# Head 0 of the expert search: eight indices found from the best eight of each side ahead of the whole search

## Chip, cores and metric

The kernel runs on one core of one Trainium2 chip. The metric is the device time of one execution in microseconds, as the median of several runs. One execution was also taken with the hardware profiler; the rows below come from that one.

## What is computed

One transformer layer on 512 tokens of width 1024 in float32: a mixer of two kinds of attention, and then a retrieval of single-neuron experts (PEER). The part that the change touches is the retrieval. For each token and each of 8 heads it takes the 16 best keys on each of two sides, the 16 best sums of the 256 pairs, and gathers the experts' rows from two tables of 16384 rows:

```python
def body(xb):                                   # xb: 128 tokens
    q = (xb @ w_q).reshape(PEER_TOKEN_BLOCK, PEER_HEADS, 2, PEER_HALF_DIM)
    sc = jnp.einsum('thpd,hpkd->thpk', q, sub_keys).astype(jnp.float32)
    s1, i1 = lax.top_k(sc[:, :, 0], PEER_TOPK)
    s2, i2 = lax.top_k(sc[:, :, 1], PEER_TOPK)
    cand = (s1[..., :, None] + s2[..., None, :]).reshape(PEER_TOKEN_BLOCK, PEER_HEADS, -1)
    cidx = (i1[..., :, None] * PEER_N_KEYS + i2[..., None, :]).reshape(PEER_TOKEN_BLOCK, PEER_HEADS, -1)
    top_s, pos = lax.top_k(cand, PEER_TOPK)
    eidx = jnp.take_along_axis(cidx, pos, axis=-1)
    g = jax.nn.softmax(top_s, axis=-1).astype(xb.dtype)
    u_sel = jnp.take(u_tab, eidx, axis=0)
    hid = jax.nn.gelu(jnp.einsum('thkd,td->thk', u_sel, xb), approximate=False) * g
    v_sel = jnp.take(v_tab, eidx, axis=0)
    return jnp.einsum('thk,thkd->td', hid, v_sel)
```

## The kernel before

The 512 tokens are four tiles of 128 tokens, one token per partition. With 8 heads each that makes 32 heads n (`HEADS`), eight per tile. The program has three parts.

**First part**, the pieces in `BEFORE`: projection, attention and output projection of tile 0, its second norm, and the queries and keys of its first heads. **Second part**, heads 0 to 7 (tile 0, "hosted"): the experts of each head are gathered one column c of 16 at a time, a u row by `gather_u` into one of 4 places of `u_ring` and a v row by `gather_v` into one of 4 places of `v_ring`; VectorE makes a dot of u with the normed tokens (`dot`, L1457), ScalarE the gelu, and VectorE adds the scaled v row to h (`add_row`, L1493). Between these steps the pieces in `AFTER` are woven in: the remaining queries and keys of tile 0, then norm, projections and attention of tiles 1 to 3 and their queries. The order on each engine is written out by the program from one list; the engines meet in semaphores. **Third part**, heads 8 to 31: u and v rows of an expert lie side by side in a third table, 8 KB each, and one gather per column (`gather_row`, L665) brings both for 128 tokens; VectorE makes the dots and TensorE adds the scaled v rows in PSUM.

The search of a head on VectorE: `topk_first` takes from the 128 scores of each side the best eight (MAX8, L1382), replaces them by a very small number (L1385), finds their places (L1387), takes the next eight and their places (L1390, L1393), and adds the 16 by 16 pairs in `cand` (L1394). `topk_second` does the same on the 256 sums, splits each place into a side-0 and a side-1 part (L1421, L1422), picks the key numbers by a comparison with `iota_i`, a product and a sum (L1425, L1431, L1435), and writes the expert numbers to `eidx` (L1440). Each step counts `topk_step` up, and later steps wait for its count. For head 0 the whole search (`topk_all`) stands ahead of the first dot; for later heads its steps are woven between the dots of the head before.

GpSimd issues the gathers in this order: it waits for head 0's expert numbers (`numbers_of(0)`), issues u0 to u3, then u4, v0, u5, v1 and so on. Gather u(c) with c of 4 or more waits for dot c-3, since it takes that place of the ring. VectorE's program at the start of the second part reads: dot 0, dot 1, norm1 of tile 1 (L1225, which waits for ScalarE's root, and L1226, which writes `xs`), dot 2, two copies of the transposed tile (L1234), dot 3, and then the first half of head 1's search.

In the same stretch TensorE makes the queries of heads 1 to 7. Each head's query weights are a slab of 1 MB in one of two places of `w_ring` (`load_slab`, L589, issued by SyncE when TensorE has used up the slab that lay there). Per head: 16 matmuls with the slab (L720), two transposes (L749), key scores of the head before (L842). ScalarE copies each result out of PSUM (L1061, L1064, L1072). Behind head 4's query TensorE transposes tile 1 (L702), for which it needs the `xs` of VectorE's norm1, and norm1 needs ScalarE's Square (L983) and root (L986); these stand in ScalarE's program behind the copies of head 4's query. ScalarE's exponential of head 0's gates (L1107) stands ahead of them.

Of the kernel before, what the change touches and what calls it, by code (L numbers as in the profile page):

```python
# [25 lines left out]
U32 = mybir.dt.uint32  # L26
# [4 lines left out]
P = 128  # L31
# [46 lines left out]
def build(nc, x, x_cols, g1_cols, first_halves, slabs, f_cols, b_f, lambda_q1, lambda_k1, lambda_q2, lambda_k2, subln_g,  # L78
# [10 lines left out]
    PH = sub_cols.shape[1] // (2 * P)  # L89
    TOPK = 16  # L90
    SLAB = HALF_BANK
    CHUNK = 64
    slopes = [2.0 ** (-8.0 * (i + 1) / NDH) for i in range(NDH)]
    HEADS = TILES * PH
# [243 lines left out]
    with ExitStack() as ctx:  # L338
# [74 lines left out]
        cand_w = onehot[:, 0:TOPK, :]  # L413
        picked = sb("picked", [P, 2, TOPK])
        eidx = [sb(f"eidx{i}", [P, TOPK], I32) for i in range(3)]
        gneg = sb("gneg", [P, 1])
        gexp = sb("gexp", [P, TOPK])
        fin_inv = sb("fin_inv", [P, 1])
# [79 lines left out]
        pv_done = sem("pv_done")  # L498
        o_drained = sem("o_drained")
        topk_step = sem("topk_step")  # L500
        gexp_done = sem("gexp_done")
        u_in = [sem(f"u_in{i}") for i in range(U_RING)]
        v_in = [sem(f"v_in{i}") for i in range(V_RING)]
# [124 lines left out]
        @block.gpsimd  # L628
        def _(pool):
            nc.gpsimd.memset(ident[:, :], 0.0).then_inc(pool_const, 1)  # L630
            nc.gpsimd.memset(causal[:, :], 0.0).then_inc(pool_const, 1)
            nc.gpsimd.iota(fin[:, 0:SEQ].bitcast(I32), pattern=[[1, SEQ]], base=-(SEQ - P), channel_multiplier=-1).then_inc(pool_const, 1)
            nc.gpsimd.iota(iota_i[:, :], pattern=[[1, TOPK]], base=0, channel_multiplier=0).then_inc(pool_const, 1)
            pool.wait_ge(pool_const, 4)
            nc.gpsimd.affine_select(out=ident[:, :], in_=ident[:, :], compare_op=ALU.not_equal, fill=1.0,
                                    base=0, pattern=[[-1, P]], channel_multiplier=1).then_inc(pool_const, 1)

            nc.gpsimd.affine_select(out=causal[:, SEQ - P:SEQ], in_=causal[:, SEQ - P:SEQ], compare_op=ALU.is_ge, fill=-BIG,
                                    base=0, pattern=[[-1, P]], channel_multiplier=1).then_inc(pool_const, 1)

            def gather_u(n, c):
                if n or c >= U_RING:
                    pool.wait_ge(dot_done, TOPK * n + c + 1 - U_RING)
                nc.gpsimd.indirect_dma_start(  # L644
                    out=u_ring[:, c % U_RING, :], out_offset=None, in_=peer_u[0],
                    in_offset=bass.IndirectOffsetOnAxis(ap=eidx[n % 3][:, c:c + 1], axis=0)).then_inc(u_in[c % U_RING], 16)

            def gather_v(n, c):
                if n or c >= V_RING:
                    pool.wait_ge(v_used, TOPK * n + c + 1 - V_RING)  # L650
                nc.gpsimd.indirect_dma_start(  # L651
                    out=v_ring[:, c % V_RING, :], out_offset=None, in_=peer_v[0],
                    in_offset=bass.IndirectOffsetOnAxis(ap=eidx[n % 3][:, c:c + 1], axis=0)).then_inc(v_in[c % V_RING], 16)

            def gather_row(n, c):

                place, lap = row_place(n, c)
                if lap > 1:
                    pool.wait_ge(v_used, HOSTED + place_rows[place][lap - 2] + 1)
                elif place == EARLY_ROWS:  # L660
                    pool.wait_ge(dot_done, HOSTED)
                    pool.wait_ge(v_used, HOSTED)
                elif place == RING:
                    pool.wait_ge(mm_full, len(MM))
                nc.gpsimd.indirect_dma_start(  # L665
                    out=row_mem[place], out_offset=None, in_=peer_uv,
                    in_offset=bass.IndirectOffsetOnAxis(ap=eidx[n % 3][:, c:c + 1], axis=0)).then_inc(row_in[place], 16)

            def numbers_of(n):

                pool.wait_ge(topk_step, TK * n + TK_IDX)

            numbers_of(0)
            for c in range(COLS):
                gather_u(0, c)
            for n in range(PH * HOSTS):
                for c in range(TOPK):
                    ahead = TOPK * n + c + COLS
                    if ahead < HOSTED:
                        if ahead % TOPK == 0:  # L680
                            numbers_of(n + 1)
                        gather_u(ahead // TOPK, ahead % TOPK)
                    gather_v(n, c)
            for n in range(PH * HOSTS, HEADS):
                numbers_of(n)
                for c in range(TOPK):
                    gather_row(n, c)
# [496 lines left out]
        def _(dve):  # L1184
# [185 lines left out]
            def after_topk(n, k):  # L1370

                dve.wait_ge(topk_step, TK * n + k)

            def topk_first(n, par):

                dve.wait_ge(*emptied(("keys", n % PH, n // PH)))
                def after(k):
                    after_topk(n, k)

                s1 = [key_sc[:, n, 0:K1], key_sc[:, n, K1:2 * K1]]  # L1380
                for q in range(2):
                    nc.vector.max(tk_v[:, q, 0:8], s1[q]).then_inc(topk_step, 1)  # L1382
                for q in range(2):
                    after(q + 1)
                    nc.vector.match_replace(tk_w[:, q, :], tk_v[:, q, 0:8], s1[q], -HUGE).then_inc(topk_step, 1)  # L1385
                for q in range(2):
                    nc.vector.max_index(tk_i[:, q, 0:8], tk_v[:, q, 0:8], s1[q]).then_inc(topk_step, 1)  # L1387
                for q in range(2):
                    after(q + 3)
                    nc.vector.max(tk_v[:, q, 8:16], tk_w[:, q, :]).then_inc(topk_step, 1)  # L1390
                for q in range(2):
                    after(q + 7)
                    nc.vector.max_index(tk_i[:, q, 8:16], tk_v[:, q, 8:16], tk_w[:, q, :]).then_inc(topk_step, 1)  # L1393
                nc.vector.tensor_tensor(out=cand[:, :, :], in0=tk_v[:, 0, :].unsqueeze(2).broadcast_to([P, TOPK, TOPK]),  # L1394
                                        in1=tk_v[:, 1, :].unsqueeze(1).broadcast_to([P, TOPK, TOPK]),
                                        op=ALU.add).then_inc(topk_step, 1)

            def topk_second(n, par, part):
# [14 lines left out]
                elif part == 2:  # L1413
                    after(13)
                    nc.vector.max(top_v[:, 8:16], wf_).then_inc(topk_step, 1)
                elif part == 3:
                    after(15)
                    nc.vector.max_index(top_p[:, 8:16], top_v[:, 8:16], wf_).then_inc(topk_step, 1)
                elif part == 4:
                    after(16)  # L1420
                    nc.vector.tensor_scalar(top_hl[:, 0, :], top_p[:, :], 4, None, ALU.logical_shift_right).then_inc(topk_step, 1)  # L1421
                    nc.vector.tensor_scalar(top_hl[:, 1, :], top_p[:, :], 15, None, ALU.bitwise_and).then_inc(topk_step, 1)  # L1422
                elif part == 5:
                    after(18)
                    nc.vector.tensor_tensor(out=onehot[:, :, :], in0=top_hl[:, :, :].rearrange("p a b -> p (a b)").unsqueeze(2).broadcast_to([P, 2 * TOPK, TOPK]),  # L1425
                                            in1=iota_i[:, :].unsqueeze(1).broadcast_to([P, 2 * TOPK, TOPK]),
                                            op=ALU.is_equal).then_inc(topk_step, 1)
                elif part == 6:
                    after(19)
                    oh = onehot[:, :, :].rearrange("p (a b) c -> p a b c", a=2)  # L1430
                    nc.vector.tensor_tensor(out=oh, in0=oh, in1=tk_i[:, :, :].unsqueeze(2).broadcast_to([P, 2, TOPK, TOPK]),  # L1431
                                            op=ALU.mult).then_inc(topk_step, 1)
                elif part == 7:
                    after(20)
                    nc.vector.tensor_reduce(picked[:, :, :].rearrange("p a b -> p (a b)"), onehot[:, :, :], AX, ALU.add).then_inc(topk_step, 1)  # L1435
                else:
                    after(21)
                    if n >= 3:
                        dve.wait_ge(v_used, TOPK * (n - 2))
                    nc.vector.scalar_tensor_tensor(out=eidx[n % 3][:, :], in0=picked[:, 0, :], scalar=float(K1), in1=picked[:, 1, :],  # L1440
                                                   op0=ALU.mult, op1=ALU.add).then_inc(topk_step, 1)
                    nc.vector.tensor_scalar(gneg[:, :], top_v[:, 0:1], -1.0, None, ALU.mult).then_inc(topk_step, 1)  # L1442

# [232 lines left out]
```

## Time and profile before

| | |
|---|---|
| runs | 1573.56, 1575.78, 1581.61 us; median 1575.78 |
| profiled execution | 1577.52 us, of which the span of the core is 1575.3 us |
| busy in the span | TensorE 1260.2 us, VectorE 1139.9, GpSimd 767.2, ScalarE 443.6 |
| DMA | 594.92 MB, mean 378 GB/s |

The profile names the engines PE (TensorE), PEld (its weight loads), DVE (VectorE), ACT (ScalarE), POOL (GpSimd) and SP (SyncE). The page cuts the span in 40 slices of 39.4 us; its rows give for each slice a busy share or a rate. The timeline gives an engine's instructions with start and duration, and in brackets how long the engine had been idle before and what ended that. The table of stretches gives for a stretch of time each engine's busy time, the granted clock of TensorE as a share of full speed, the busy share of the 16 DMA engines, and their rate. The table of DMA queues gives for a stretch what each queue moved: q1 holds SyncE's loads, q0 GpSimd's gathers.

### The profile page before, as it was taken

The numbers are of one execution on the slowest core, as the hardware profiler recorded it, in microseconds if no ns is written. First come the engines' busy times: TensorE is split into PE (matmuls) and PEld (weight loads), VectorE is DVE, ScalarE is ACT, GpSimd is POOL, SyncE is SP. The second block draws the span as 40 slices with busy tenths as digits, with TensorE's granted clock in tenths as the row PEclk, the third lists the DMA queues.
The fourth block names the chain that finished last, engine by engine and source line by source line (L and its number), as shares of the span: only waits on it lengthen the run. The fifth ranks groups of instructions, "written<-read, shape, count | busy, mean of one in ns | idle before, by whom it ended". The sixth has DMA issues, their size and how long they took to land.

```text
span 1575.3 us, 12952 instructions
## 1 busy us (share of the span) xinstructions
PE 1260.2 (80%) x3685; PEld 659.3 (42%) x3685; DVE 1139.9 (72%) x2676; ACT 443.6 (28%) x1062; POOL 767.2 (49%) x650
## 2 busy tenths in 40 slices
PE   9986998987685846989987768687777877777777
PEld 7665564566452523444433323233332333333233
DVE  3247889999999887666676677667666676666664
ACT  3332234444443212212222222221222222222222
POOL 0025657776575673444554444444453454555440
PEclk9997998998887877999999989989999998999999
DMA  9378989998888899999999999999999999999995
GB/s 380 144 284 325 383 323 348 360 364 330 275 289 323 309 382 387 420 421 422 421 422 421 422 422 422 421 421 422 422 421 421 422 422 421 421 422 421 421 422 209
DMA packets 101613, 594.92 MB, mean 378 GB/s; under 512 B 11688, under 2 KB 11688, under 8 KB 46248
## 3 DMA queue, kind: packets, MB, share of 16 engines
q0 software_dynamic: 92160, 536.91, 84.9%
q1 hardware_dynamic: 9384, 57.19, 9.2%
q8 instruction: 31, 0.51, 0.1%
q14 instruction: 38, 0.31, 0.0%
HBM read 591.96 MB, written 2.10 MB: 377 GB/s over the span
## 4 chain that ended last, share of the span: by engine, by line
DMA 34%; DVE 13%; PE 13%; ACT 2%; POOL 2%; issue 2%; POOLq 0%; DVEq 0%
PE acc L934 11%; DMA mix_mem<-in_peer_uv_dram,eidx 8%; DMA map_mem<-in_peer_uv_dram,eidx 7%; DMA v_ring<-in_peer_uv_dram,eidx 6%; DMA v_all<-in_peer_uv_dram,eidx 4%; DMA u_ring<-in_peer_uv_dram,eidx 3%; DMA act_mem<-in_peer_uv_dram,eidx 3%; DMA w_ring<-in_peer_uv_dram,eidx 3%; PE mm L728 1%; DVE v_all L1465 1%; DVE map_mem L1465 1%; DVE v_ring L1465 1%; DVE u_ring L1465 1%; ACT diag L1118 1%; DVE mix_mem L1465 1%
## 5 line engine op out<-in xcount | busy, mean ns | idle before, releaser
L644 POOL DMA_INDIRECT u_ring<-in_peer_u_dram,eidx x128 | 158.0, 1234 | 197.1 <-DVE gneg L1442 98.8
L1111 ACT ACTIVATE gel<-hid 128x4 f32<-128x4 f32 x126 | 25.8, 205 | 742.7 <-DVE hid L1465 698.6
L651 POOL DMA_INDIRECT v_ring<-in_peer_v_dram,eidx x128 | 152.3, 1190 | 72.0 <-issue 33.2
L934 PE MATMUL acc<-v_all,diag 128*128 128x512 f32 x240 | 118.3, 639 | 64.1 <-ACT diag L1118 64.1
L1493 DVE SCALAR_TENSOR_TENSOR h<-v_ring,coef,h 128x1024 f32<-128x1024 f32 x128 | 164.3, 1283 | 5.9 <-DMA v_ring<-in_peer_v_dram,eidx 2.6
L1457 DVE CUSTOM_DVE_ANT_0 u_ring<-u_ring,hn 128x1024 f32<-128x1024 f32 x128 | 156.1, 1219 | 10.7 <-DMA u_ring<-in_peer_u_dram,eidx 10.2
L934 PE MATMUL acc<-u_ring,diag 128*128 128x512 f32 x240 | 121.3, 653 | 27.8 <-ACT diag L1118 27.8
L934 PE MATMUL acc<-v_ring,diag 128*128 128x512 f32 x240 | 118.6, 641 | 30.2 <-ACT diag L1118 30.2
L934 PE MATMUL acc<-map_mem,diag 128*128 128x512 f32 x240 | 116.1, 629 | 28.2 <-ACT diag L1118 28.2
L1118 ACT ACTIVATE diag<-ident,coef 128x128 f32<-128x128 f32 x376 | 121.1, 390 | 30.6 <-DVE coef L1483 21.5
L728 PE MATMUL mm<-act_mem,w_ring 128*128 128x384 f32 x352 | 126.8, 519 | 2.6 <-issue 1.9
L665 POOL DMA_INDIRECT map_mem<-in_peer_uv_dram,eidx x60 | 72.4, 1206 | 88.6 <-PE acc L934 81.6
L665 POOL DMA_INDIRECT u_ring<-in_peer_uv_dram,eidx x60 | 68.4, 1140 | 89.4 <-PE acc L934 81.8
L665 POOL DMA_INDIRECT v_all<-in_peer_uv_dram,eidx x60 | 71.2, 1187 | 83.1 <-PE acc L934 76.3
L665 POOL DMA_INDIRECT v_ring<-in_peer_uv_dram,eidx x60 | 69.6, 1161 | 76.2 <-PE acc L934 69.5
L1465 DVE CUSTOM_DVE_ANT_0 map_mem<-map_mem,hn 128x1024 f32<-128x1024 f32 x60 | 72.9, 1225 | 45.9 <-DMA map_mem<-in_peer_uv_dram,eidx 45.9
L934 PEld LDWEIGHTS acc<-v_all,diag 128*128 128x128 f32 x240 | 47.9, 205 | 128.8 <-issue 95.6
L934 PE MATMUL acc<-act_mem,diag 128*128 128x512 f32 x168 | 82.6, 638 | 23.5 <-ACT diag L1118 23.5
L1465 DVE CUSTOM_DVE_ANT_0 u_ring<-u_ring,hn 128x1024 f32<-128x1024 f32 x58 | 70.4, 1224 | 42.4 <-DMA u_ring<-in_peer_uv_dram,eidx 42.4
L1465 DVE CUSTOM_DVE_ANT_0 v_all<-v_all,hn 128x1024 f32<-128x1024 f32 x60 | 72.8, 1223 | 38.7 <-DMA v_all<-in_peer_uv_dram,eidx 38.6
L1465 DVE CUSTOM_DVE_ANT_0 v_ring<-v_ring,hn 128x1024 f32<-128x1024 f32 x58 | 70.3, 1223 | 38.3 <-DMA v_ring<-in_peer_uv_dram,eidx 38.3
L934 PE MATMUL acc<-w_ring,diag 128*128 128x512 f32 x168 | 79.6, 618 | 22.1 <-ACT diag L1118 22.1
(264 smaller groups left out, 2346.5 us busy)
## 6 DMA issues: line engine op xcount, KB each, us to landing
w_ring<-in_slabs_dram SPq DMA_DIRECT2D x37, 1024.0 KB
v_ring<-in_slabs_dram SPq DMA_DIRECT2D x6, 1024.0 KB, 10.7
u_ring<-in_slabs_dram SPq DMA_DIRECT2D x4, 1024.0 KB, 10.9
h<-in_x_dram SPq DMA_DIRECT2D x4, 512.0 KB, 6.9
u_ring<-in_peer_u_dram,eidx POOLq DMA_INDIRECT x128
v_ring<-in_peer_v_dram,eidx POOLq DMA_INDIRECT x128
out_dram<-fin SPq DMA_DIRECT2D x3, 512.0 KB, 7.8
w_ring<-in_first_halves_dram SPq DMA_DIRECT2D x2, 512.0 KB, 4.6
```

What stands on the lines that cost most here:

```text
L644: nc.gpsimd.indirect_dma_start(out=u_ring[:, c % U_RING, :], out_offset=None, in_=peer_u[0], in_offset=bass.IndirectOffsetOnAxis(ap=eidx[n ...
L651: nc.gpsimd.indirect_dma_start(out=v_ring[:, c % V_RING, :], out_offset=None, in_=peer_v[0], in_offset=bass.IndirectOffsetOnAxis(ap=eidx[n ...
L665: nc.gpsimd.indirect_dma_start(out=row_mem[place], out_offset=None, in_=peer_uv, in_offset=bass.IndirectOffsetOnAxis(ap=eidx[n % 3][:, c:c ...
L728: last = nc.tensor.matmul(bk[:, 0:n], w[:, c, q * P:(q + 1) * P], actT[:, c, 0:n], start=(c == 0), stop=(c == KC - 1))
L934: last = nc.tensor.matmul(acc[half][:, :], diag[:, c % COLS, :], v_row(n, c)[:, half * BANK:(half + 1) * BANK], start=first, stop=(n % PH ...
L1111: nc.scalar.activation(gel[:, par, g0:g0 + COLS], hid[:, par, g0:g0 + COLS], ACT.Gelu).then_inc(gelu_done, 1)
L1118: nc.scalar.activation(diag[:, c, :], ident[:, :], ACT.Copy, scale=coef[:, par, g0 + c:g0 + c + 1]).then_inc(diag_done, 1)
L1457: nc.vector.tensor_tensor_reduce(out=u_ring[:, c % U_RING, :], in0=u_ring[:, c % U_RING, :], in1=hn[:, :], scale=1.0, scalar=0.0, op0=ALU. ...
L1465: nc.vector.tensor_tensor_reduce(out=u_row(n, c), in0=u_row(n, c), in1=hn[:, :], scale=1.0, scalar=0.0, op0=ALU.mult, op1=ALU.add, accum_o ...
L1493: nc.vector.scalar_tensor_tensor(out=ht, in0=v_ring[:, c % V_RING, :], scalar=coef[:, par, c:c + 1], in1=ht, op0=ALU.mult, op1=ALU.add).th ...
```

## The change

Head 0 gets a second, smaller search, `eight_first`, ahead of the rest of the whole one. The best 8 of the 256 sums come from the best 8 of each side, so the 64 sums of those give the same eight; it finds the eight expert numbers from them and writes them to columns 0 to 7 of `eidx[0]`. To have the places of the best eight of each side, `topk_first` now finds them (MAX_INDEX) ahead of the replacement, for every head. The whole search goes on behind it as before and writes columns 8 to 15. GpSimd waits for a semaphore of its own (`first_eight`) before u0, and for the whole search of head 0 only before u8. Six small tiles are added in SBUF.

```diff
+            def eight_first():
+                def sides(ap, last):
+                    return ap.unsqueeze(last).broadcast_to([P, EIGHT, EIGHT])
+                cf = first_cand[:, :, :].rearrange("p a b -> p (a b)")
+                link(nc.vector.tensor_tensor(out=first_cand[:, :, :], in0=sides(tk_v[:, 0, 0:EIGHT], 2), in1=sides(tk_v[:, 1, 0:EIGHT], 1),
+                                             op=ALU.add))
+                link(nc.vector.max(first_v[:, :], cf))
+                link(nc.vector.max_index(first_p[:, :], first_v[:, :], cf))
+                nc.vector.tensor_scalar(first_hl[:, 0, :], first_p[:, :], 3, None, ALU.logical_shift_right).then_inc(dve_chain, 1)
+                chain[0] += 1
+                link(nc.vector.tensor_scalar(first_hl[:, 1, :], first_p[:, :], EIGHT - 1, None, ALU.bitwise_and))
+                link(nc.vector.tensor_tensor(out=first_hot[:, :, :], ..., op=ALU.is_equal))
+                hot = first_hot[:, :, :].rearrange("p (a b) c -> p a b c", a=2)
+                link(nc.vector.tensor_tensor(out=hot, in0=hot, in1=tk_i[:, :, 0:EIGHT].unsqueeze(2).broadcast_to([P, 2, EIGHT, EIGHT]),
+                                             op=ALU.mult))
+                link(nc.vector.tensor_reduce(first_id[:, :, :].rearrange("p a b -> p (a b)"), first_hot[:, :, :], AX, ALU.add))
+                nc.vector.scalar_tensor_tensor(out=eidx[0][:, 0:EIGHT], in0=first_id[:, 0, :], scalar=float(K1), in1=first_id[:, 1, :],
+                                               op0=ALU.mult, op1=ALU.add).then_inc(first_eight, 1)
...
                 for q in range(2):
                     after(q + 1)
+                    nc.vector.max_index(tk_i[:, q, 0:8], tk_v[:, q, 0:8], s1[q]).then_inc(topk_step, 1)
+                if n == 0:
+                    after(4)
+                    eight_first()
+                for q in range(2):
                     nc.vector.match_replace(tk_w[:, q, :], tk_v[:, q, 0:8], s1[q], -HUGE).then_inc(topk_step, 1)
                 for q in range(2):
-                    nc.vector.max_index(tk_i[:, q, 0:8], tk_v[:, q, 0:8], s1[q]).then_inc(topk_step, 1)
-                for q in range(2):
-                    after(q + 3)
+                    after(q + 5)
                     nc.vector.max(tk_v[:, q, 8:16], tk_w[:, q, :]).then_inc(topk_step, 1)
...
-            numbers_of(0)
+            pool.wait_ge(first_eight, 1)
             for c in range(COLS):
                 gather_u(0, c)
             for n in range(PH * HOSTS):
                 for c in range(TOPK):
                     ahead = TOPK * n + c + COLS
                     if ahead < HOSTED:
+                        if ahead == EIGHT:
+                            numbers_of(0)
...
-                    nc.vector.scalar_tensor_tensor(out=eidx[n % 3][:, :], in0=picked[:, 0, :], scalar=float(K1), in1=picked[:, 1, :],
+                    lo = EIGHT if n == 0 else 0
+                    nc.vector.scalar_tensor_tensor(out=eidx[n % 3][:, lo:], in0=picked[:, 0, lo:], scalar=float(K1), in1=picked[:, 1, lo:],
                                                    op0=ALU.mult, op1=ALU.add).then_inc(topk_step, 1)
```

The order of VectorE's instructions at the start of head 0's search, before (`tk_v` holds the best values of both sides, `tk_i` their places, `tk_w` the scores with the best eight replaced):

```order
L1382 MAX tk_v<-store 128x8 x2
L1385 MATCH_REPLACE tk_w<-tk_v,store 128x128 x2
L1387 MAX_INDEX tk_i<-tk_v,store 128x8 x2
L1390 MAX tk_v<-tk_w 128x8 x2
L1393 MAX_INDEX tk_i<-tk_v,tk_w 128x8 x2
```

The same place in the changed program:

```order
L1416 MAX tk_v<-store 128x8 x2
L1419 MAX_INDEX tk_i<-tk_v,store 128x8 x2
L1391 TENSOR_TENSOR first_cand<-tk_v 128x64
L1393 MAX first_v<-first_cand 128x8
L1394 MAX_INDEX first_p<-first_v,first_cand 128x8
L1395 TENSOR_SCALAR first_hl<-first_p 128x8
L1397 TENSOR_SCALAR first_hl<-first_p 128x8
L1398 TENSOR_TENSOR first_hot<-first_hl,iota_i 128x128
L1402 TENSOR_TENSOR first_hot<-first_hot,tk_i 128x128
L1404 TENSOR_REDUCE first_id<-first_hot 128x16
L1405 SCALAR_TENSOR_TENSOR eidx<-first_id 128x8
L1424 MATCH_REPLACE tk_w<-tk_v,store 128x128 x2
```

The index searches have moved ahead of the replacements, and nine instructions stand between.

GpSimd's gathers at the start of the second part, before, with what each waits for:

```order
L644 DMA u_ring<-in_peer_u_dram,eidx 128x1024 [waits topk_step]
L644 DMA u_ring<-in_peer_u_dram,eidx 128x1024 x3
L644 DMA u_ring<-in_peer_u_dram,eidx 128x1024 [waits dot_done]
L651 DMA v_ring<-in_peer_v_dram,eidx 128x1024
```

The same place in the changed program, with the gather u8 as the last row:

```order
L652 DMA u_ring<-in_peer_u_dram,eidx 128x1024 [waits first_eight]
L652 DMA u_ring<-in_peer_u_dram,eidx 128x1024 x3
L652 DMA u_ring<-in_peer_u_dram,eidx 128x1024 [waits dot_done]
L659 DMA v_ring<-in_peer_v_dram,eidx 128x1024
...
L652 DMA u_ring<-in_peer_u_dram,eidx 128x1024 [waits dot_done,topk_step]
```

The wait for the whole search has moved from u0 to u8; the order of the gathers is the same. The programs of TensorE, ScalarE and SyncE read as before.

## Rows read from the trace of the kernel before

**Rows 1.** The page's slices of the span: DMA rate per slice.

```profile
GB/s 380 144 284 325 383 323 348 360 364 330 275 289 323 309 382 387 420 421 422 421 422 421 422 422 422 421 421 422 422 421 421 422 422 421 421 422 421 421 422 209
```

**Rows 2.** Table of stretches: start:end, length, busy of five engines, clock, DMA share, rate.

```profile
113.89:145.62 31.73, 20.77 (x86) 17.47 (x86) 23.23 (x59) 12.28 (x25) 15.20 (x14) 0.77 0.90 342
...
582.00:1575.00 993.00, 780.56 (x1716) 335.74 (x1716) 679.64 (x1684) 232.82 (x615) 455.08 (x385) 0.93 0.99 411
```

**Rows 3.** Timeline of VectorE from 93 to 128 us: start, duration, instruction, [idle before].

```profile
93.68 0.49 DVE L1382 MAX8 tk_v<-store 128x8 f32<-128x128 f32 x2 [1.46 <-ACT store L1072]
...
94.67 0.28 DVE L1387 FIND_INDEX8 tk_i<-tk_v,store 128x8 uint32<-128x128 f32 x1
...
96.04 0.40 DVE L1394 TENSOR_TENSOR cand<-tk_v 128x256 f32<-128x256 f32 x1
...
100.46 0.69 DVE L1435 TENSOR_REDUCE picked<-onehot 128x32 f32<-128x512 f32 x1
101.18 0.17 DVE L1440 SCALAR_TENSOR_TENSOR eidx<-picked 128x16 int32<-128x16 f32 x1
...
108.50 1.23 DVE L1457 CUSTOM_DVE_ANT_0 u_ring<-u_ring,hn 128x1024 f32<-128x1024 f32 x1 [7.08 <-DMA u_ring<-in_peer_u_dram,eidx]
...
113.89 0.16 DVE L1225 RECIPROCAL stat<-stat 128x1 f32<-128x1 f32 x1 [2.90 <-ACT stat L986]
...
127.58 1.21 DVE L1457 CUSTOM_DVE_ANT_0 u_ring<-u_ring,hn 128x1024 f32<-128x1024 f32 x1
```

**Rows 4.** Timeline of GpSimd: the first two gathers.

```profile
101.64 1.09 POOL L644 DMA_INDIRECT u_ring<-in_peer_u_dram,eidx  x1 [98.84 <-DVE gneg L1442]
103.03 0.94 POOL L644 DMA_INDIRECT u_ring<-in_peer_u_dram,eidx  x1 [0.30 <-issue]
```

**Rows 5.** Timeline of ScalarE from 106 to 112 us.

```profile
106.33 1.28 ACT L1107 ACT_TABLE_LOAD   x1
...
109.78 0.38 ACT L1061 ACTIVATE mix_mem<-mm 128x256 f32<-128x256 f32 x1 [1.43 <-PE mm L720]
...
111.04 1.06 ACT L983 ACTIVATE xs<-h 128x1024 f32<-128x1024 f32 x1
```

**Rows 6.** Timeline of TensorE from 106 to 122 us.

```profile
106.12 3.62 PE L720 MATMUL mm<-w_ring,act_mem 128*128 128x256 f32 x16
...
114.90 1.97 PE L702 MATMUL mm<-ident,xs 128*128 128x128 f32 x8 [4.23 <-DVE xs L1226]
116.66 5.55 PE L720 MATMUL acc<-w_ring,act_mem 128*128 128x256 f32 x16
```

**Rows 7.** Timeline of SyncE: three of its slab loads.

```profile
100.94 0.33 SPq L589 DMA_DIRECT2D w_ring<-in_slabs_dram  x1
105.39 0.33 SPq L589 DMA_DIRECT2D w_ring<-in_slabs_dram  x1
...
122.25 0.33 SPq L589 DMA_DIRECT2D w_ring<-in_slabs_dram  x1
```

**Rows 8.** DMA queues, 102.4 to 105.3 us: packets, MB, share of 16 engines' time.

```profile
q1 hardware_dynamic: 131, 0.98, 86.5%
```

**Rows 9.** DMA queues, 105.5 to 109 us (first row) and 109 to 113.2 us.

```profile
q0 software_dynamic: 282, 1.04, 88.0%
...
q1 hardware_dynamic: 134, 1.03, 58.4%
q0 software_dynamic: 200, 0.73, 43.8%
```

**Rows 10.** DMA queues, 122.3 to 125.3 us (first row) and 125.3 to 129.3 us.

```profile
q0 software_dynamic: 337, 1.22, 102.1%
...
q1 hardware_dynamic: 139, 1.05, 63.0%
```

**Rows 11.** Table of stretches, columns as in rows 2: the clock's fall and return.

```profile
113.50:114.00 0.50, 0.00 (x0) 0.00 (x0) 0.11 (x1) 0.48 (x2) 0.50 (x1) 0.74 1.02 426
120.50:121.00 0.50, 0.50 (x4) 0.44 (x3) 0.50 (x4) 0.00 (x0) 0.50 (x1) 0.93 1.03 410
```

More of the change, by code:

```diff
@@ L91, in build @@
     SLAB = HALF_BANK
+    EIGHT = 8
     CHUNK = 64
@@ L415, in build @@
         eidx = [sb(f"eidx{i}", [P, TOPK], I32) for i in range(3)]
+        first_cand = sb("first_cand", [P, EIGHT, EIGHT])
+        first_v = sb("first_v", [P, EIGHT])
+        first_p = sb("first_p", [P, EIGHT], U32)
+        first_hl = sb("first_hl", [P, 2, EIGHT], U32)
+        first_hot = sb("first_hot", [P, 2 * EIGHT, EIGHT])
+        first_id = sb("first_id", [P, 2, EIGHT])
         gneg = sb("gneg", [P, 1])
@@ L500, in build @@
         topk_step = sem("topk_step")
+        first_eight = sem("first_eight")
         gexp_done = sem("gexp_done")
@@ L1372, in after_topk @@
                 dve.wait_ge(topk_step, TK * n + k)
+            def eight_first():
[9 more added lines that the diff above has]
+                link(nc.vector.tensor_scalar(first_hl[:, 1, :], first_p[:, :], EIGHT - 1, None, ALU.bitwise_and))
+                link(nc.vector.tensor_tensor(out=first_hot[:, :, :],
+                                             in0=first_hl[:, :, :].rearrange("p a b -> p (a b)").unsqueeze(2).broadcast_to([P, 2 * EIGHT, EIGHT]),
+                                             in1=iota_i[:, 0:EIGHT].unsqueeze(1).broadcast_to([P, 2 * EIGHT, EIGHT]), op=ALU.is_equal))
+                hot = first_hot[:, :, :].rearrange("p (a b) c -> p a b c", a=2)
[4 more added lines that the diff above has]
+                                               op0=ALU.mult, op1=ALU.add).then_inc(first_eight, 1)
             def topk_first(n, par):
```

## The prediction

> **What bounds the kernel now.** I read the slices of the page first [rows 1]. From slice 17 on the 16 DMA engines move about 420 GB/s without a break: that is the part from 582 us on, in which rows of 8 KB per token and expert are gathered for heads 8 to 31 (411 GB/s over 993 us [rows 2]). It carries 63% of the span and the change doesn't touch it. So whatever the change does in front of it arrives at the end only as a shift of its start, and it arrives in full: bytes and order of that part stay.
>
> The change lies between 93.68 and about 110 us. There the second thing to read is who waits. VectorE searches head 0 from 93.68 to 101.4 [rows 3]; GpSimd then issues four u gathers, the first at 101.64 [rows 4]; VectorE idles 7.08 us until the first of them has landed and makes its first dot at 108.50 [rows 3]. This looks like 7 us on the path. But read on: after the second dot VectorE waits another 2.90 us, until 113.89, for ScalarE's root for norm1 of tile 1 [rows 3]. That root follows ScalarE's Square of 111.04, the Square follows the copies of head 4's queries, and the first of these, at 109.78, waited 1.43 us for TensorE [rows 5]. TensorE multiplies head 4's slab from 106.12 and then idles 4.23 us, until 114.90, for xs, which VectorE makes right behind that root [rows 6]. So the path here is: query slabs in TensorE, copies in ScalarE, Square and root, xs in VectorE, transposes in TensorE. The first dots are on it nowhere.
>
> The third thing is what TensorE's slabs depend on. Each slab of 1 MB is loaded into one of two places of w_ring when the slab two before it is used up; SyncE issued them at 100.94, 105.39 and 122.25, among others [rows 7]. The slab issued at 100.94 is head 4's, used from 106.12 on [rows 6, 7]. That leaves 5.2 us from issue to use.
>
> **The change, part by part.**
>
> *Nine more VectorE instructions.* The two maxima stay at 93.68; the two index searches follow at once (0.28 us each), so the new work starts near 94.8. It works on 8 to 128 elements a partition; rows exist for 16, 256 and 512: 0.17, 0.40 and 0.69 us [rows 3]. The slope between them gives about 0.25 for 128 and 0.2 for 64. So: three instructions on 128 elements 0.75; add and maximum on 64 at 0.2 and their index search, which loads its eight values first, 0.3, together 0.7; three on 8 to 16 elements 0.5; seven waits for the instruction before at 0.03 (L1435 ends at 101.15, L1440 starts at 101.18 [rows 3]) 0.2. That is 2.15 us. Bounds: 1.5 us (nine at 0.17) and 3.6 us (nine at 0.40). I take 2.15, since most of the nine are nearer in size to the 16 elements. The first eight indices are there near 97.1, and GpSimd's first gather starts some 0.3 us later (as 101.64 stands to 101.35 now), near 97.4: 4.2 us earlier. The others follow at its pace of 1.3 to 1.4 us [rows 4].
>
> *The rest of the search* ends 2.15 us later, near 103.5. Who waits for that: VectorE's own first dot (the gather took 101.64 to 108.50, 6.9 us, so it lands near 104.3: the delay is hidden behind it); ScalarE's exponential of head 0, which is reached at 106.33 [rows 5] (2.8 us in hand); the indices 8 to 15, wanted by GpSimd only after dot 4, which starts at 127.58 [rows 3]. Nothing waits. Cost 0; if the cover of the landing were gone, 2.15 us would still lie in front of the 2.90 us wait for ScalarE.
>
> *The earlier dots.* Dots 0 and 1 now lie between about 104.3 and 107 and not 108.5 and 111. Dot 2 stands behind norm1 of tile 1 in VectorE's program. So the idle time only moves: less before the first dot, more (2.90 + 4.2 us) before the reciprocal L1225. Gain 0. The gathers u4, v0, u5, v1 also go 4 us earlier; dot 4 starts at 127.58 without a wait now [rows 3], so this brings 0 as well.
>
> *The wait of GpSimd* for the whole search, moved from before gather 0 to before gather u8: queued behind it are u8 itself and v4; the search will have ended 24 us before. 0.
>
> *What the earlier gathers collide with.* This is the term that I expect to count. Two stretches of the DMA queues show what a slab does with and without gathers in flight. The slab issued at 100.94 had the engines for itself: 0.98 MB of it flow from 102.4 to 105.3, 4.4 us after its issue it is there [rows 8]. The next one, issued at 105.39, met four gathers, the first issued 3.75 us earlier: from 105.5 to 109 the slab queue moved nothing at all, the gathers 1.04 MB; only from 109 to 113.2 did it move 1.03 MB, beside 0.73 MB of gathers [rows 9]. That is 7.8 us from issue to the end. Before, it does no harm: head 5's slab is wanted behind the xs wait, at 116.66 [rows 6]. With the change the first gather is issued near 97.4, that is 3.5 us ahead of the slab of 100.94, and the three others stand to it as they stood to the next one. So head 4's slab should take what head 5's took: 100.94 + 7.8 = 108.7 us, and TensorE, which wants it at 106.1, idles 2.6 us. Another slab behind gathers was issued at 122.25, moved nothing until 125.3 and 1.05 MB until 129.3: 7.05 us [rows 7, 10], which would make the wait 1.9 us. Head 3's slab, issued a slab's pace (4.4 us) before 100.94, is through by 101: the first gather's data, which flow from 105 now [rows 8, 9], 3.4 us after its issue, would come near 100.8.
>
> If the slab shared the engines from the start, it would flow from 1.5 us after its issue (102.4 against 100.94 [rows 7, 8]) at the rate of the shared stretch, 1.03 MB in 4.2 us [rows 9]: there at 106.6, a wait of 0.5 us. The 3.5 us without a byte of it, seen twice, are nearer; I take 2.6 and keep 0.5 as a rival. The Trainium skill (DMA: Bandwidth & Descriptors, section on queues, rings and completion order) states the rule behind that rival: each DMA engine goes round robin between the queues that have work, a packet at a time. The trace agrees in the shared stretch and not in the 3.5 us before it [rows 9].
>
> *What the wait does further.* It stands on the path: copies, Square, root, xs and TensorE's next transposes all come 2.6 us later, and so does everything behind. Head 5's slab (issued at 105.39 as before, now in second place behind head 4's) is wanted near 119.3 and should be there by 113 to 114. TensorE's clock: it fell from full to half 3.1 us after the idle stretch began at 110.67 (the granted clock of 113.5 to 114 is 0.74, a mean of full and half [rows 11]), so 2.6 us alone are likely too short; if it falls all the same, head 4's 16 matmuls take 5.55 and not 3.62 us, as head 5's did [rows 6]: +1.9 us.
>
> Sum against the profiled execution: its time 1577.5 (span 1575.3 and 2.2 around it) + 0 (search) + 0 (dots) + 2.6 (slab) = 1580.1. It lies 1.7 us above the median of the runs, 1575.8, so the median to expect is 1578.4. The scatter of the runs shown, 1573.6 to 1581.6, is larger than the effect; a measurement of this kernel can tell about 0.5% (7.9 us) from no change, and the whole forecast is a third of that.
>
> **The rivals.**
>
> *A, the slab is in time* (0 us, 1575.8): the gathers start later than I think (new work 3.6 us, first gather at 98.9) or DMA takes them in another order. For it: head 4's slab has 0.8 us in hand now. Against: with 98.9 the gathers are still in flight at 102.4, when the slab's data would begin.
>
> *B, the slab shares from the start*: wait 0.5 us, 1576.3, worked out above. For it: the shared stretch of rows 9. Against: 3.5 us with nothing from the slab queue there, and 3 us in rows 10. It decides if the slab's first bytes flow by 103.
>
> *C, the head start arrives* (-4.2 us, 1571.6): it needs norm1 of tile 1 to hang on the dots. Against: what ended that wait is ScalarE, not a dot [rows 3]. Even the whole of it is 0.27%.
>
> *D, slower by over 0.5%*: the wait pulls TensorE's clock down and holds it. The stretch 113.89 to 145.62 has 20.8 us of TensorE work at a mean granted clock of 0.77 [rows 2]; with 0.50 throughout, the same work takes 20.8 x 0.77 / 0.50 = 32 us, 11 more. With the 2.6 that is up to +13.8, in the middle some +9: 1585. It decides, against the 7.9 us, once half of those 11 us are lost. Against: the clock came back between 120.5 and 121 [rows 11], 6 us after TensorE had begun again.
>
> *E, it doesn't do what it says*: the eight of the first gather are found no earlier, since each of the nine costs some 0.7 us, as the 512-element ones do. Then gathers start near 101.6 as now, the search ends 6 us later, near 107.5, and the first dots still end inside the wait for ScalarE: 0, 1575.8.
>
> **How the numbers follow.** Forecast (slab late by 1.9 to 2.7, with or without 1.9 of clock: +1.9 to +4.6) 0.62; A 0.15; B 0.10; C 0.04; D 0.05; E 0.04. All but D lie inside 0.5%. From D and the scatter: slower 0.06; from C and the scatter: faster 0.02; within 0.5%: 0.92. Range: from C's 1571.6 to the forecast's upper end, 1575.8 + 4.6 = 1580.4, and some 2.5 above it for the half of D that begins there: 1572 to 1583.
>
> **What would show it.** Right: the first gather near 97.4; a wait of TensorE of about 2.6 us before head 4's query matmuls near 106, ended by the w_ring DMA; VectorE's wait before its first dot shrunk to about 1 us and the one before L1225's counterpart grown to about 9.7; first row gather near 585 and not 582. Wrong: no wait of TensorE at 106 (A, B), or a start of the row part 4 us earlier (C), or half clock beyond 125 (D).

## The result, and the profile after

Over 21 runs each, the changed kernel took 1583.23 us (1578.09 to 1586.92) and the kernel before 1577.73 us (1573.40 to 1582.81): ratio 1.0032, 95% interval 1.0022 to 1.0042, that is 5.0 us more, between 3.5 and 6.6 (the two medians lie 5.5 us apart). It is slower, clear of the noise, and by less than the 0.5% set as the bound. One name ahead of the result is wrong: the norm that is called tile 1's (the reciprocal L1225 at 113.89) is that of tile 2; the second group's tiles are normed in the order 2, 3, 1. Its place and its waits are as told.

The profiled execution of the changed kernel has a span of 1576.8 us, only 1.5 us over that of before. The rows below say where the rest is. The searches and the first gathers are where they were put. Timeline of VectorE, the counterpart of rows 3 (start, duration, instruction, idle before):

```profile
93.70 0.49 DVE L1416 MAX8 tk_v<-store 128x8 f32<-128x128 f32 x2 [1.46 <-ACT store L1082]
...
94.74 0.23 DVE L1391 TENSOR_TENSOR first_cand<-tk_v 128x64 f32<-128x64 f32 x1
...
96.85 0.17 DVE L1405 SCALAR_TENSOR_TENSOR eidx<-first_id 128x8 int32<-128x8 f32 x1
...
103.51 0.17 DVE L1478 SCALAR_TENSOR_TENSOR eidx<-picked 128x8 int32<-128x8 f32 x1
...
104.28 1.23 DVE L1495 CUSTOM_DVE_ANT_0 u_ring<-u_ring,hn 128x1024 f32<-128x1024 f32 x1 [0.55 <-DMA u_ring<-in_peer_u_dram,eidx]
...
119.93 0.16 DVE L1235 RECIPROCAL stat<-stat 128x1 f32<-128x1 f32 x1 [13.14 <-ACT stat L996]
```

The first dot starts at 104.28 and not at 108.50. But the wait for ScalarE's root, 2.90 us in rows 3, is now 13.14 us and ends 6.0 us later than before. GpSimd (rows 4) and SyncE (rows 7):

```profile
97.30 1.09 POOL L652 DMA_INDIRECT u_ring<-in_peer_u_dram,eidx  x1 [94.50 <-DVE eidx L1405]
98.69 0.94 POOL L652 DMA_INDIRECT u_ring<-in_peer_u_dram,eidx  x1 [0.30 <-issue]
```

```profile
100.96 0.33 SPq L597 DMA_DIRECT2D w_ring<-in_slabs_dram  x1
```

Timeline of TensorE (rows 6):

```profile
101.73 3.69 PE L730 MATMUL mm<-w_ring,act_mem 128*128 128x256 f32 x16
...
110.40 5.38 PE L730 MATMUL mm<-w_ring,act_mem 128*128 128x256 f32 x16 [4.05 <-issue]
...
120.94 1.57 PE L712 MATMUL mm<-ident,xs 128*128 128x128 f32 x8 [4.23 <-DVE xs L1236]
122.30 4.87 PE L730 MATMUL acc<-w_ring,act_mem 128*128 128x256 f32 x16
```

Head 4's query started at 106.12 in rows 6 without a wait; now TensorE idles 4.05 us in front of it, and its 16 matmuls take 5.38 instead of 3.62 us. The profile names no releaser ("issue"), so the DMA queues must be read. The first two rows are 101.1 to 104.4 us, the next two 104.4 to 109 us, the last two 109 to 110.4 us; a second fence has TensorE's clock in three stretches (last but two of the columns).

```profile
q0 software_dynamic: 291, 1.07, 90.3%
...
q1 hardware_dynamic: 2, 0.01, 1.7%
...
q1 hardware_dynamic: 143, 1.07, 55.4%
q0 software_dynamic: 230, 0.86, 46.4%
...
q1 hardware_dynamic: 65, 0.50, 84.4%
q0 software_dynamic: 31, 0.08, 14.0%
```

```profile
109.00:109.50 0.50, 0.00 (x0) 0.00 (x0) 0.00 (x0) 0.00 (x0) 0.36 (x1) 1.00 0.95 393
...
111.00:111.50 0.50, 0.50 (x3) 0.39 (x2) 0.00 (x0) 0.00 (x0) 0.32 (x1) 0.67 0.92 385
...
112.00:114.00 2.00, 2.00 (x6) 1.62 (x5) 0.00 (x0) 0.00 (x0) 0.00 (x0) 0.50 1.01 414
```

It is the picture of rows 9, moved onto the next slab: 3.3 us in which the slab issued at 100.96 gets 0.01 MB and the gathers 1.07 MB, then both share. The rows don't tell when head 4's slab is complete: q1 moves 1.57 MB between 104.4 and 110.4, more than the one slab of 1.05 MB (1024 KB), since head 5's, issued at 105.45, stands in the same queue behind it. Another record of the trace does. Each slab load counts its semaphore up in 16 steps, and the trace has the time of each (none of the views shown here prints them). For head 4's slab they come from 108.37 to 110.31, only 9 of them by 109.0, and TensorE's first matmul with the slab starts at 110.40, 0.09 us behind the last.

The granted clock is still full from 109 to 109.5 and falls to half between 111 and 111.5, when TensorE has been multiplying again for 0.6 to 1.1 us.

The delay is carried on: the first row gather of the third part starts 4.5 us later.

```profile
582.43 1.22 POOL L665 DMA_INDIRECT v_all<-in_peer_uv_dram,eidx  x1 [0.30 <-issue]
```

```profile
586.92 1.21 POOL L673 DMA_INDIRECT v_all<-in_peer_uv_dram,eidx  x1 [0.30 <-issue]
```

(first fence before, second after). From there to the end of the span it is 992.9 us before and 989.9 us after. This part has the same program in both, and in the ten executions of the experiments below, with the same program there, it took from 989.5 us (e6) to 994.3 us (e5). So the 3 us by which the profiled execution of after was shorter there lie in the scatter between executions: the 1.5 us of the spans understate, and the 5.0 us of the runs agree with the 4.5 us at the start of the third part.

### The profile page after: what moved, and what is told of

It is laid out like the page before. It is cut to its first block, busy times and chain, and to the rows that moved or that the text cites. A ratio compares the mean times of both kernels' runs of the same rounds, so it can differ in the third digit from the quotient of the medians.

```text
span 1576.8 us, 12963 instructions
## 1 busy us (share of the span) xinstructions
PE 1269.1 (80%) x3685; PEld 663.0 (42%) x3685; DVE 1141.3 (72%) x2686; ACT 443.4 (28%) x1062; POOL 775.2 (49%) x650
## 4 chain that ended last, share of the span: by engine, by line
DMA 35%; PE 14%; DVE 10%; POOL 2%; ACT 2%; issue 1%; DVEq 0%
PE acc L944 12%; DMA u_ring<-in_peer_uv_dram,eidx 9%; DMA v_ring<-in_peer_uv_dram,eidx 7%; DMA map_mem<-in_peer_uv_dram,eidx 5%; DMA mix_mem<-in_peer_uv_dram,eidx 5%; DMA act_mem<-in_peer_uv_dram,eidx 4%; DMA v_all<-in_peer_uv_dram,eidx 3%; DMA w_ring<-in_peer_uv_dram,eidx 1%; DVE v_ring L1503 1%; PE mm L738 1%; DVE u_ring L1503 1%; ACT diag L1128 1%; DVE map_mem L1503 1%; DVE v_all L1503 1%; DVE mix_mem L1503 1%
## 5 line engine op out<-in xcount | busy, mean ns | idle before, releaser
L944 PE MATMUL acc<-v_all,diag 128*128 128x512 f32 x240 | 122.6, 659 | 65.8 <-ACT diag L1128 65.8
L944 PE MATMUL acc<-v_ring,diag 128*128 128x512 f32 x240 | 115.4, 626 | 18.7 <-ACT diag L1128 18.7
L673 POOL DMA_INDIRECT u_ring<-in_peer_uv_dram,eidx x60 | 73.9, 1232 | 86.7 <-PE acc L944 78.4
L944 PE MATMUL acc<-act_mem,diag 128*128 128x512 f32 x168 | 90.0, 686 | 26.3 <-ACT diag L1128 26.3
```

The source lines that it names most:

```text
L673: nc.gpsimd.indirect_dma_start(out=row_mem[place], out_offset=None, in_=peer_uv, in_offset=bass.IndirectOffsetOnAxis(ap=eidx[n % 3][:, c:c ...
L944: last = nc.tensor.matmul(acc[half][:, :], diag[:, c % COLS, :], v_row(n, c)[:, half * BANK:(half + 1) * BANK], start=first, stop=(n % PH ...
```

## The experiments

Each is compared with the kernel before on its own chip, with 9 to 12 runs of its own against 25 to 35.

### e1: the gathers wait for the whole search again

```diff
             pool.wait_ge(first_eight, 1)
+            numbers_of(0)
             for c in range(COLS):
```

> The changed kernel, with GpSimd waiting for head 0's whole search before the first gather again; the nine VectorE instructions and the earlier index searches stay. Slab theory (the time goes where head 4's query slab meets gathers that are in flight): gathers start near 103.8, the slab of 100.95 has the engines for itself, TensorE doesn't wait at 106, ratio to before 1.000 within 0.001, that is 0 to +1 us. Rival (the added VectorE work or the other order of the search costs the time): as the changed kernel, ratio 1.003, +5 us.

Measured: 1574.74 us against 1576.28, ratio 0.9997 (0.9981 to 1.0013). The first dot of this execution starts at 111.80, three microseconds later than before. TensorE:

```profile
106.41 3.62 PE L731 MATMUL mm<-w_ring,act_mem 128*128 128x256 f32 x16
115.22 1.97 PE L713 MATMUL mm<-ident,xs 128*128 128x128 f32 x8 [4.26 <-DVE xs L1237]
```

No wait in front of head 4's query. The nine instructions and the moved index searches cost nothing that can be measured (the interval ends at +2 us), nor do dots 3 us late: they use up the wait in front of the norm (its reciprocal starts at 114.22 without one). The cause is in the early gathers.

### e3 and e10: the slab out of the gathers' way

```diff
         def slab_place(n):
+            if n == APART:                      # head 4's query slab
+                return 3, N_IN + N_OUT - 1      # second half of v_ring
...
+            load_slab(APART)                    # SyncE, ahead of the loop
             for n in range(N_IN + N_OUT + 2, len(slab_order) - 2):
...
             def gather_v(n, c):
+                if n == 0 and c == 2:
+                    pool.wait_ge(mm_full, slab_last_use[slab_order[APART]] + 1)
```

> The changed kernel with all four early gathers, but head 4's query slab goes to the second half of v_ring, free since the output projection, and is issued near 86.5 us, ahead of the gathers; v2 waits for its use. Slab theory: no wait of TensorE at 106, norm1 at 113.9 as before, and the whole head start of 4.2 us disappears in VectorE's wait for ScalarE's root: ratio 1.000 within 0.001, 0 us. Rival (the early gathers harm something else, or the search does): 1.003. Second rival (the head start is worth its 4.2 us once the slab is out of its way): 0.9975.

Measured: 1577.87 against 1576.28 us, ratio 1.0005 (0.9993 to 1.0017). TensorE and VectorE of e3:

```profile
106.27 3.62 PE L743 MATMUL mm<-v_ring,act_mem 128*128 128x256 f32 x16
```

```profile
104.36 1.22 DVE L1508 CUSTOM_DVE_ANT_0 u_ring<-u_ring,hn 128x1024 f32<-128x1024 f32 x1 [0.64 <-DMA u_ring<-in_peer_u_dram,eidx]
114.04 0.16 DVE L1248 RECIPROCAL stat<-stat 128x1 f32<-128x1 f32 x1 [7.18 <-ACT stat L1009]
```

In e3 SyncE issues the slab at 86.50. All four gathers are early and the first dot starts at 104.36, as in the changed kernel; the slab's wait is gone, and so is the loss. The head start sits in VectorE's wait for the root: 7.18 us, which is 2.90 of rows 3 and the 4.2 us gained. Since the effect is small, I took both kernels again beside each other.

> The changed kernel once more, beside e10 on the same chip. Ratio to before 1.002 to 1.004 (it was 1.0032).

> e3 once more (the changed kernel with head 4's slab out of the gathers' way), beside e9 on the same chip. Slab theory: ratio to before 1.000 within 0.0012, and some 0.003 under e9. Rival (the difference lay in the sessions): as e9.

Measured: the changed kernel 1581.07 us, ratio 1.0033 (1.0022 to 1.0043); with the slab apart 1575.31 us, ratio 1.0000 (0.9988 to 1.0012); before 1575.21 us. The intervals don't touch, and a gain of 4.2 us (ratio 0.9973) lies outside e10's too. This is the pair that settles the cause. TensorE in e9 (first row), with a wait of 3.24 us and head 4's matmuls at full clock (it falls near 119.6, in the wait for xs), and in e10 (second), with no wait:

```profile
111.32 3.69 PE L730 MATMUL mm<-w_ring,act_mem 128*128 128x256 f32 x16 [3.24 <-issue]
...
108.08 3.62 PE L743 MATMUL mm<-v_ring,act_mem 128*128 128x256 f32 x16
```

### e2: two gathers early, two behind the whole search

```diff
             for c in range(COLS):
+                if c == 2:
+                    numbers_of(0)
                 gather_u(0, c)
```

> The changed kernel, with only gathers u0 and u1 ahead of the wait for the whole search; u2 and u3 behind it. Slab theory: the slab meets half of the gather bytes (1.05 MB and not 2.1), so it lands some 2.5 us earlier than with four (TensorE's wait 4.05 us there): wait of 1 to 2 us, without or with little of the clock's fall; ratio 1.000 to 1.001, +0 to +2 us. Rival (any early gather holds the slab for as long, since it is the start of its packets that is late): wait still 3 us or more, ratio 1.002 to 1.003. Dots 0 and 1 come as early as in the changed kernel; if the head start were worth something it would show here as a ratio under 0.999.

Measured: 1579.71 against 1576.28 us, ratio 1.0019 (1.0007 to 1.0031), some 3 us. This execution ran 1.6 us late already at 93 us; the slab is issued at 102.55. The DMA queues from 103 to 105 us and from 105 to 108 us, and TensorE:

```profile
q0 software_dynamic: 203, 0.76, 95.9%
...
q1 hardware_dynamic: 115, 0.93, 79.5%
q0 software_dynamic: 57, 0.18, 14.5%
```

```profile
109.70 3.69 PE L732 MATMUL mm<-w_ring,act_mem 128*128 128x256 f32 x16 [1.72 <-issue]
```

With half of the gather bytes the slab waits until those are through (nothing of it from 103 to 105), then has the engines nearly to itself. The wait is 1.72 us, as the slab theory had it (its rival had 3 us or more), and dose and effect go together: four gathers 4.05 and 3.24 us, two 1.72 us, none 0. The ratio missed: it came out above the 1.000 to 1.001 expected, nearer to the rival's 1.002; its interval reaches from 1 to 5 us. See what stays open, below. Dots 0 and 1 are as early as in the changed kernel and bring nothing.

### e4: the norms of heads 4 and 5 ahead of the query (on the kernel before)

```diff
         for hd in range(PH if g == 0 else PH - LATE_HEADS):
+            if ahead_of:                        # hd is 4 or 5 of the first group
+                queries += [("norm1", g + 1, GROUPS[g + 1][hd - PH // 2 + 1])]
             queries += [("query", g, 2 * hd)]
...
-                queries += normed(g + 1, GROUPS[g + 1][hd - PH // 2 + 1])
+                queries += [("xT", g + 1, GROUPS[g + 1][hd - PH // 2 + 1])]
```

> The kernel before with one thing moved: the norms that ScalarE and VectorE make during heads 4 and 5 (Square, root, xs) stand ahead of that head's query instead of behind it; the transposes stay. It tests what the path is in this stretch. Theory (path is query, copies, Square, root, xs, transposes): TensorE's two waits of 4.2 us for xs shrink to 1 to 2 us each, some 5 us earlier from 150 us on, ratio 0.996 to 0.998. Rival (the path is VectorE's dots, from the landing of the first gather on): ratio 1.000.

Measured: 1574.66 against 1576.28 us, ratio 0.9988 (0.9976 to 0.9999). It is faster, if only just clear of 1, so Square, root and xs were on the path, but by 2 us and not 5. TensorE:

```profile
111.38 0.41 PE L752 MATMUL acc<-ident,mix_mem 128*128 128x128 f32 x2 [1.07 <-ACT mix_mem L1064]
112.12 1.09 PE L705 MATMUL mm<-ident,xs 128*128 128x128 f32 x8 [0.33 <-DVE xs L1229]
114.24 5.38 PE L723 MATMUL acc<-w_ring,act_mem 128*128 128x256 f32 x16 [1.03 <-issue]
121.66 0.41 PE L752 MATMUL mm<-ident,mix_mem 128*128 128x128 f32 x2 [1.60 <-ACT mix_mem L1064]
...
130.09 0.68 PE L845 MATMUL acc<-subkT,qyT 128*128 128x128 f32 x4 [3.14 <-DVE act_mem L1237]
```

The two waits of 4.23 us for xs shrank to 0.33 us (the second stands at 122.40), but four new ones came in: for ScalarE's copies, which now queue behind the norm (1.07 and 1.60), for head 5's slab, which meets the gathers in the way of rows 9 (1.03), and for VectorE's copies behind its dots (3.14).

### e5, e6, e7: the early norms with and without the early eight

e5 is the changed kernel with the edits of e3 and e4; e6 that of e2 and e4; e7 the kernel before with those of e3 and e4.

> The changed kernel with head 4's slab out of the gathers' way (as in e3) and the norms of heads 4 and 5 ahead of the query (as in e4, which gave 0.9988 alone). There the first dots and their gathers had moved onto the path: VectorE waited 1.33 us for u3 and TensorE 1.03 us for head 5's slab. Theory (the head start is worth nothing only because the wait for ScalarE's root covers it): 2 to 4 us under e4, ratio 0.996 to 0.998. Rival (the head start is worth nothing at all): as e4, 0.9988.

> As e5, but head 4's slab stays where it was and only u0 and u1 are gathered early. TensorE's wait of 1.7 us for the slab comes back and the early norms take their 2 us off: ratio 0.999 to 1.000 by the slab theory; as e5 by its rival (two early gathers do no harm).

> The kernel before with both moves of e5 (head 4's slab in v_ring, early norms) but without the eight first indices. It tells what the early eight are worth in e5. Theory: the slab's move alone gives nothing here, so as e4, 0.9988, and 2 us slower than e5. Rival: equal to e5, then the gain of e5 comes from the slab.

Measured against 1577.47 us: e5 1574.61, ratio 0.9977 (0.9962 to 0.9992); e6 1576.50, 0.9998 (0.9980 to 1.0016); e7 1576.05, 0.9990 (0.9974 to 1.0006). e5 and e7 can't be told apart by their times; TensorE's start on the projections of the second group tells more (e5 first, e7 second):

```profile
146.86 7.73 PE L754 MATMUL mm<-act_mem,w_ring 128*128 128x384 f32 x16 [1.87 <-issue]
```

```profile
146.89 7.51 PE L744 MATMUL mm<-act_mem,w_ring 128*128 128x384 f32 x16 [1.87 <-issue]
```

They are level with each other, and 1.4 us ahead of e4's 148.24; at the first row gather they stand at 580.54 (e5) and 580.00 (e7), and e4 at 579.93, so nothing of the 1.4 us is left there. The ratio of e5 lies where I expected it, but the reason I gave isn't shown: its interval also holds e4's 0.9988 and e7's 0.9990, and the traces have no sign that the early eight bring anything even with the norms early, since VectorE then waits 5.64 us for the root at 111.06 (3.96 us in e7). Whether e5 is faster than e4 or e7 stays open. e6 has the slab's wait back (1.81 us), and by its median it loses what the norms gave.

### e8: the third norm too

```diff
+            if g + 1 < len(GROUPS) and hd == PH - 1:
+                queries += [("norm1", g + 1, GROUPS[g + 1][0])]
...
-        ps = normed(g, tiles[0])
+        ps = normed(g, tiles[0]) if g == 0 else [("xT", g, tiles[0])]
```

> e5 with the third norm too (that of the first tile of the second group, now behind head 7's query) ahead of head 7's query. TensorE's wait of 4.26 us for its xs near 143 should shrink to 1 to 2 us: 2 to 3 us under e5, ratio to before 0.9955 to 0.998. Rival (VectorE's dots or the projections' first slab take over): as e5, 0.9977.

Measured: 1568.06 against 1575.21 us, ratio 0.9957 (0.9940 to 0.9973): 7 us faster than before and 13 us faster than the changed kernel on the same chip (e9). The same start as above, in an execution that was 1.6 us later than e5 at 112 us and ends up ahead:

```profile
145.02 5.40 PE L756 MATMUL mm<-act_mem,w_ring 128*128 128x384 f32 x16 [1.36 <-issue]
```

That is 1.8 us before e5, or 3.5 us with the late start taken off; at the first row gather it is 4.9 us before e5 (575.60 against 580.54). TensorE no longer waits for the third xs (4.26 us in e5), but for ScalarE's copies of head 7 (3.25 us). It is the fastest version of the study. It still contains the early eight; a version with the three norms and without them was not run.

## Why the prediction was right, and where it was off

**The path.** Right: the first dots were nowhere on it. e3 and e10 kept the whole head start and gained nothing; e1 made the dots later than before and lost nothing. Rival C falls.

**The nine instructions.** 2.15 us forecast; the search now ends 2.3 us later (103.51 against 101.18). First gather at 97.4 forecast, 97.30 measured; first dot 104.3, measured 104.28. 64 elements took 0.23 us where I had put 0.2, 128 took 0.29 where I had 0.25; the slope that I named gives 0.22 and 0.28, so I had rounded it down. Rival E falls, and A with it, since TensorE waits.

**The slab.** The forecast took head 5's slab of rows 9 as the pattern for head 4's, since the gathers would stand to it in the same way. The mechanism held: 3.3 us of nearly nothing (3.5 forecast), then a shared stretch. Rival B, sharing from the start, would have given a wait of 0.5 us; measured were 4.05 and 3.24 us.

**The term that was mis-sized is the wait itself: 2.6 us forecast, 4.05 us measured** (3.24 in e9). The step that was off is "100.94 + 7.8 = 108.7 us, and TensorE idles 2.6 us". It counted the slab as there when the queue had moved about 1 MB. But SyncE issued head 6's slab at 109.77, so the last of the bytes of rows 9 need not be head 5's, and the load isn't done when they have flowed. The 16 steps of the semaphore tell it: in the trace of before, those of head 5's slab come from 113.28 to 114.35, the last 8.96 us after the issue. With that figure in place of 7.8 the same sum gives 109.9 us and a wait of 3.8 us. Measured from issue to last step: 9.35 us in after (the steps are spread over 1.9 us), 8.6 in e9, 7.1 in e2 with half of the gathers. In each of them TensorE starts 0.09 us behind the last step. The 0.8 us that the forecast gave head 4's slab in hand was read in the same way and is also too large: 11 of its 16 steps are recorded, up to 105.82, 0.3 us ahead of the matmuls.

**The clock.** I had left the fall out of the forecast, because 2.6 us of idling were shorter than the 3.1 us after which it fell in rows 11, and kept 1.9 us as the bound. That comparison doesn't carry: in after it fell 4.8 us after TensorE had gone idle (at 106.35), when it had begun again, and in e9 it didn't fall over a wait of 3.24 us. What is measured is the cost: at half clock head 4's matmuls took 5.38 us in after, 1.76 more; in e9 they took 3.69. In after the wait and the clock together are 5.8 us and show as 6.0 us at the root (119.93 against 113.89). 1.1 us of it come back by the next norm (131.32 against 126.37), since the transposes and head 5's query then run partly at full clock, 1.57 instead of 1.97 and 4.87 instead of 5.55 us. The start of the third part is 4.5 us late, the runs 5.0 us. Rival D is the same mechanism held on for 30 us; it did not hold: the mean granted clock from 110 to 160 us is 0.76 in before and in after.

**The numbers.** "Within 0.5%" at 0.92 was right, but it was a wide mark: rivals A, B, C and E would have met it too. The size was half right: 2.6 us forecast, 5.0 measured, just over the forecast's own upper end of +4.6 us. The range reached from -3.8 to +7.2 us about the three runs shown of before, and 5.0 lies in it, in the part that was added for rival D; the time itself, 1583.23, ends up 0.2 us above the stated 1583.0, because the kernel before too came out 2 us higher in the longer series.

**What stays open.** In after the delay is there in full when attention starts (226.37 against 221.77 in before). In e9 it is 3.0 us against e10 at the start of attention (224.91 against 221.93, both executions level at 93.96) and 7.2 us at the first row gather (first row e9, second e10):

```profile
588.96 1.22 POOL L673 DMA_INDIRECT v_all<-in_peer_uv_dram,eidx  x1 [0.30 <-issue]
...
581.72 1.22 POOL L686 DMA_INDIRECT v_all<-in_peer_uv_dram,eidx  x1 [0.30 <-issue]
```

So 4 us more arose in between. e2 shows the same against e10, 2.1 us growing to 5.8. The kernels without the slab's wait, before, e1, e3 and e10, took 359.8 to 360.8 us over that stretch, after 360.6, e9 364.1 and e2 363.5. I didn't find what adds it; the mean granted clock from 230 to 300 us is 0.86 in e9 and 0.90 in e10, but that is one execution each and no test. So it is shown that the loss needs early gathers that meet head 4's slab. That the wait and the clock behind it make up all of the 5 us is not shown: the 5.8 us above are one execution's, and in e9 the wait accounts for 3 of its 7 us.

## What to carry to other kernels

A transfer that starts earlier meets other transfers: before moving gathers forward, list the loads that will then be issued into them, with the time that each has until its first use. A wait that is on nobody's path (7 us in front of the first dot) is worth nothing, and it is found by reading on to the next wait of the same engine and what ends that; here the engine's next wait ended by a chain over TensorE and ScalarE, and moving that chain's norms (e8) gave what the shorter search could not. When a landing decides, don't take it from a queue's bytes: the next load may already stand in the same queue. Take the last step of the load's semaphore or the start of a user that waited for it.

## What the runs showed of the hardware

A slab load issued while gathers were in flight moved next to nothing for 3.5 to 4.0 us from its issue (rows 9, rows 10, after, e9; 2.7 us in e2 with two gathers), until 1.2 to 1.3 of the four gathers' 2.1 MB (rows 9, after and e9) or 0.97 of the two gathers' 1.05 MB (e2) had flowed. With free engines the first bytes of one flowed 1.0 us after its issue (101.90, and most from 102.5, in before; 87.46 after 86.50 in e3). Only after the silence did both share, the slab at 0.23 to 0.26 MB per us (rows 9, rows 10, after). The Trainium skill (DMA: Bandwidth & Descriptors, section on queues, rings and completion order) has each engine go round robin between queues that have work; the shared stretch agrees, the silence before it does not by itself follow from it. Whether the load's descriptors come late or stand behind gather descriptors already taken, no run here tells.

The 16 steps by which a slab's semaphore counts up were spread over 1.1 to 1.9 us where gathers were in flight (108.37 to 110.31 in after, 110.17 to 111.23 in e9, 108.31 to 109.61 in e2, 113.28 to 114.35 in before), and TensorE, where it waited for the slab, started 0.09 us behind the last (after, e9, e2).
